# A retention layer's 24 input strips: value strips ahead of key and query strips

## The reference

```
z = h @ w_in                                   # 1024 -> 6144: q, k, v and gate of 4 heads
q = rope(z[q]); k = rope(z[k]) / 16            # 256 features a head
v, gate = z[v], z[gate]                        # 512 features a head
per chunk:  a = (q k^T) * decay;  o = a v + (q * q_dec) S;  S = c_dec * S + (k * k_dec)^T v
y = silu(gate) * groupnorm(o);  out = y @ w_out
```

## Time and profile before

| what | value |
|---|---|
| runs shown | 977.67, 977.97, 979.68 us; median 977.97 us |
| profiled execution, its own time | 976.55 us |
| its span | 974.3 us |
| mean granted TensorE clock | 0.995 of full speed |
| PE, PEld busy | 952.8, 883.3 us |
| DVE, ACT, POOL busy | 592.0, 430.1, 37.6 us |
| first to last transposition of values (L1089) | starts from 497.6 to 663.3 us |

### The profile page before, as it was taken

The page is one execution under the profiler, slowest core; times in us unless marked ns, Lnnn a source line. Parts: engine busy times, 40 slices in busy tenths (PEclk is TensorE's granted clock), DMA queues, the critical chain, the costliest instruction groups (busy, mean ns, idle before and its releaser), DMA issues. The chain is left out here.

```text
span 974.3 us, 17740 instructions
## 1 busy us (share of the span) xinstructions
PE 952.8 (98%) x7550; PEld 883.3 (91%) x7550; DVE 592.0 (61%) x768; ACT 430.1 (44%) x543; POOL 37.6 (4%) x68
## 2 busy tenths in 40 slices
PE   8999999899999999999999999999999999999996
PEld 8988998558999999999988978788899899999995
DVE  6866654874786653334875767676764875543443
ACT  6232224766554553333542644434344565543331
POOL 0510000000000000000001010000000000000000
PEclk9999999999999999999999999999999999999998
DMA  9987759967254445543556867675674344444411
GB/s 346 366 287 272 267 195 350 329 218 269 89 190 162 167 172 173 173 159 143 209 181 263 317 239 299 233 274 197 249 280 155 133 173 170 172 173 161 158 69 48
DMA packets 50989, 206.62 MB, mean 212 GB/s; under 512 B 3568, under 2 KB 3952, under 8 KB 35440
## 3 DMA queue, kind: packets, MB, share of 16 engines
q1 hardware_dynamic: 45504, 182.58, 52.7%
q0 software_dynamic: 5424, 23.15, 6.1%
HBM read 181.39 MB, written 24.33 MB: 211 GB/s over the span
## 5 line engine op out<-in xcount | busy, mean ns | idle before, releaser
L1289 ACT ACTIVATE wH<-raw 128x2048 fp32r<-128x2048 f32 x115 | 220.4, 1916 | 350.1 <-PE banks L630 339.6
L1669 DVE TENSOR_TENSOR wL<-raw,wH 128x2048 fp32r<-128x2048 f32 x112 | 256.6, 2291 | 191.0 <-ACT wH L1289 191.0
L628 PE MATMUL banks<-hH,wH 128*128 128x288 f32 x1152 | 346.0, 300 | 0.9 <-DVE sqacc L1754 0.5
L630 PE MATMUL banks<-hH,wL 128*128 128x288 f32 x1152 | 339.8, 295 | 0.0
L629 PE MATMUL banks<-hL,wH 128*128 128x288 f32 x1152 | 339.5, 295 | 0.0
L628 PEld LDWEIGHTS banks<-hH,wH 128*128 128x128 f32 x1152 | 217.7, 189 | 14.0 <-issue 10.5
L629 PEld LDWEIGHTS banks<-hL,wH 128*128 128x128 f32 x1152 | 216.8, 188 | 1.1 <-issue 0.7
L630 PEld LDWEIGHTS banks<-hH,wL 128*128 128x128 f32 x1152 | 216.5, 188 | 0.0
L630 PE MATMUL banks<-aH,wL 128*128 128x288 f32 x512 | 151.8, 296 | 0.0
L628 PE MATMUL banks<-aH,wH 128*128 128x288 f32 x512 | 151.3, 296 | 0.0
L629 PE MATMUL banks<-aL,wH 128*128 128x288 f32 x512 | 149.3, 292 | 0.0
(11 more groups left out here) (302 smaller groups left out, 1068.7 us busy)
## 6 DMA issues: line engine op xcount, KB each, us to landing
raw<-wst SPq DMA_DIRECT2D x119, 1024.0 KB, 4.9
cache_sb<-kcache SPq DMA_DIRECT2D x14, 1024.0 KB, 7.7
sslot<-state SPq DMA_DIRECT2D x11, 1024.0 KB, 5.9
sstate_out<-sslot POOLq DMA_DIRECT2D x11, 1024.0 KB, 5.5
raw<-vcache SPq DMA_DIRECT2D x6, 1024.0 KB, 10.6
w_area<-vcache SPq DMA_DIRECT2D x6, 1024.0 KB, 12.9
raw<-state SPq DMA_DIRECT2D x5, 1024.0 KB, 5.1
sstate_out<-raw POOLq DMA_DIRECT2D x5, 1024.0 KB, 5.4
```

Of the source, the lines that this page charges most:

```text
L628: nc.tensor.matmul(out[:, m, :], wH[:, u % 2, c], hi[:, k, :], start=first, stop=False)
L630: return nc.tensor.matmul(out[:, m, :], wL[:, u % 2, c], hi[:, k, :], start=False, stop=last)
L1289: nc.scalar.activation(wH[:, at % SPL, :], raw[:, raw_slot(at), :], ACT.Copy).then_inc(h_round, 1)
L1669: nc.vector.tensor_tensor(wL[:, at % SPL, :], raw[:, raw_slot(at), :], wH[:, at % SPL, :].bitcast(F32), ALU.subtract).then_inc(l_split, 1)
```

## The change

The order of the strips of heads 1, 2 and 3 becomes value, value, key, query. Head 0 keeps its order on PE, key, query, value, value, but DVE takes those four as p = 0, 2, 3, 1: the key, the two values, and then the query. `P_V_END`, which counts strips taken, and the two waits of PE for emptied banks (strips 4 and 5) follow. In the first four strips the head steps that do something (the clearing of `qpad`, `own_columns(0)`) and the split of strip 5 stay at the third and fourth place in DVE's order. Sizes, instructions and their number stay as they are.

```diff
 def _head_strips(h):
-    return 4 + h, h, 8 + 2 * h, 9 + 2 * h
+    values, turned = (8 + 2 * h, 9 + 2 * h), (4 + h, h)
+    return values + turned if h else turned + values
...
-P_V_END = (3, 7, 13, 19)
+
+
+FIRST_TAKEN = (0, 2, 3, 1)
+P_V_END = (2, 5, 11, 17)
...
-                pe.wait_ge(g_dve, GBUF + GD_RET + (p - 3 if p < 6 else p - 1))
+                pe.wait_ge(g_dve, GBUF + GD_RET + (1 if p == 4 else 4 if p == 5 else p - 1))
...
-            for p in range(N_RETIN):
+            for i, p in enumerate(FIRST_TAKEN + tuple(range(4, N_RETIN))):
                 s, c = S_RETIN + p, RET_ORDER[p]
-                head_step(p, 0)
-                head_step(p, 1)
+                if p >= 4:
+                    head_step(p, 0)
+                    head_step(p, 1)
                 dve.wait_ge(strip_used, s + 1)
...
-                    rotate(None, GD_RET + p, p, 16 + 2 * h + (c < NHR), lambda z: to[:, z:z + 1, :],
+                    rotate(None, GD_RET + i, p, 16 + 2 * h + (c < NHR), lambda z: to[:, z:z + 1, :],
                            at=s + SPL if p == 0 else None, src=pair(p) if p < 4 else G(p))
...
-                head_step(p, 2)
+                if i >= 3:
+                    head_step(i, 2)
                 if p == 2:
                     nc.vector.memset(qpad[:, :, :], 0.0).then_inc(r_dec, 1)
-                if p == 3:
-                    split_strip(s + 2, s + 2)
+                if i == 3:
+                    split_strip(S_RETIN + 5, S_RETIN + 5)
```

## The result

The changed kernel is slower: 984.38 us, median of 6 runs (982.90 to 984.78), against 978.25 us of the kernel before (6 runs, 976.71 to 979.68). The ratio is 1.0062, 95% interval 1.0052 to 1.0071. The forecast was 983.1, in a range of 980.0 to 985.6, slower with 0.86. The measured loss is 6.1 us, the forecast one 5.15.

A forecast was written before the change was run, and what follows sets the result against it. PE was taken to bound the kernel, with DVE's order deciding its waits at `kpad`. -0.54 + 1.60 + 2.84 + 1.25 = 5.15 us slower, on a median of 977.97, gave 983.1 us, range 980.0 to 985.6.

The forecast's parts named there:

- What bounds: PE, busy 952.8 of 974.3 us, bounds the kernel; only PE waits that go or come move the time.
- the sign: PE's idle time from 466 to 700 us grows by some 5 us; otherwise the prediction is wrong.
- The unit and the wait: On DVE, a rotation replacing a value strip adds 1.60 us; `own_columns` waiting directly behind the query's rotation adds 0.19.
- The four heads: Change in when PE gets `kpad`: head 0 gains 0.54 us; heads 1, 2, 3 lose 1.60, 2.84, 1.25.
- The clock: Rival: 2.9 us idle at head 3's `kpad` lowers PE's clock, up to 5 us more, 985 to 988; chance 0.08.
- The likeliest case: The forecast itself: DVE's order delays `kpad` in heads 1 to 3, 5.15 us slower, 983.1 us; chance 0.78.
- What was costed at nothing: ACT's high `kpad` copy (0.40 us a head), strips taken earlier, DMA queues and late splits add no time.
- That `kpad` is covered: Rival: DVE's chain has air, three value waits go and none replaces them, 2.89 us faster; chance 0.06.
- That DVE absorbs the rotations: Rival: DVE absorbs rotations of strips 7 and 12; only strips 13, 19 and waits count, about 0.7 us; chance 0.08.

The follow-up runs named there:

- the first head: Against the changed kernel, only DVE's order in head 0 stays changed; heads 1 to 3 return to key, query, value, value: 977.45 us against 977.38.
- its head alone: Three kernels against the one before, value strips first only in head 1, 2 or 3: single times 979.43, 980.32 and 979.71 us.
- the 6 matmuls: Changed kernel with 6 filling matmuls, results overwritten, ahead of PE's wait for `pad_low` in head 3: 981.75 us against 977.49 before.
- `pad_low` first: Changed kernel with `pad_low` directly behind `own_columns`, ahead of DVE's split of the next strip, in all heads: 980.49 us against 978.05 before.

## Why the prediction was right, point by point

*What bounds.* Right. All of the loss is in PE's idle time and clock. From 466 to 700 us before PE is idle for 4.7 us, and from 466 to 708 us after for 9.3, so the growth of some 5 us that was named as the sign is there; the slack of 0.54 us that was read between `pad_low` and `kpad`'s transpositions is the 0.52 that the first head gains.

*The unit and the wait.* In the changed trace the key strip of head 2 costs DVE 595.85 - 593.58 = 2.27 us, as reckoned. The step from a rotation to an instruction that waits for it is 0.59 us, against 0.37 without a wait: 0.22, and 0.19 was reckoned. DVE's rows (start us, us) in head 2:

```profile
607.50 0.45 DVE L1764 TENSOR_TENSOR qr<-sqacc 128x288 f32<-128x288 f32 x1
608.09 0.23 DVE L2053 TENSOR_TENSOR norms<-kr,norms 128x64 f32<-128x64 f32 x1
```

The Trainium skill ("VectorE: DVE Perf Modes", section "The DRAIN you can't avoid") has chained DVE instructions take the same time with a semaphore behind each as with one behind the last. Taken for waits, as the prediction takes it, it disagrees with these rows as it did with those of before. By it the sum would have been 4.8 us, by the traces it is 5.3.

*The four heads.* Reckoned -0.54, +1.60, +2.84, +1.25, together 5.15. Measured -0.52, +1.63, +2.87, +1.31, together 5.29, and each of the last three shown by itself with its head alone. That the strips taken earlier, ACT's copies and the DMA queues were put at nothing is borne out by what is left over, 0.14 us. The waits at `kpad` were forecast at 0.9, 1.9 and 2.9 us and are 1.02, 1.72 and 2.55.

*The clock.* This is the step that went otherwise. The likeliest case had no fall of the clock; the rival with it had 0.08. It falls in all four traces in which PE waits 2.5 us or more at `kpad`, and in none of the ten others. Its price is 1.58 us and not up to 5, since the fall does not last to the end of strip 20: in the changed kernel's trace the clock is back at 1.00 before 678 us. The rows named the danger (2.05 us kept the clock, a long idle stretch did not), and the chance given to it was too small. The 2.05 us row was also one execution: behind the same wait the clock fell in 8 of the 14 traces that there are now. So the number is in part luck. With the clock at its measured price the same sum would have been 5.15 + 1.58 = 6.7 us, or 984.7, which the range still held; the rival's own 985 to 988 us was too dear. The measured 6.1 us are in between 5.3 and 5.3 + 1.6 = 6.9, and the interval, 5.1 to 6.9 us, does not tell the two apart; the two traces without the fall in attention, 6.9 us apart, and the 6 matmuls do.

*What was costed at nothing.* One thing was missed beside the clock: the split of strip 20 is late by 0.50 us (PE's wait at L632), since the key's rotation is ahead of it. It ends before the wait for `kpad` does and costs nothing, but it is part of why that wait is 2.55 us and not 2.9. And ACT's copies are covered only as long as DVE's split stands beside them; with the split gone they are the next bound, as the ACT rows above show.

*The rivals.* That `kpad` is covered: no, the first head shows it alone. That DVE absorbs the rotations: no, heads 1 and 2 give 1.59 and 2.86 us.

## What to carry to other kernels

When a wait is to be removed, look at what the same engine waits for next and how much slack it has there: here 0.54 us stood behind a wait of 1.49, and that was all there was to win. Before an order is turned round, ask which of its members is dearest for the engine that must hand over (a rotation is 2.27 us on DVE, a value strip 0.67) and keep the dear ones away from the handing over. A long wait of PE can cost more than itself: here 2.55 us brought 1.6 us of low clock behind them. Put matmuls into it, if they end before the wait does, or end it sooner.

## What the runs showed of the hardware

The granted clock behind PE's waits among the retention strips: 1.00 behind 1.72 to 1.81 us at `kpad` in head 2 and behind 1.76 in head 3 (`pad_low` first), and at the 1.2 GHz level behind 2.54 to 2.56 us, in four traces of four, 1.56 to 1.63 us lost each time. Between them lies the 2.05 to 2.07 us wait in attention, which every kernel here has: behind it the clock fell in 8 of the 14 traces and stayed in 6, among them that of the kernel before. From the end of this wait to the group of matmuls at 478 us it takes 299.6 us where the clock stayed and 300.9 to 301.1 where it fell, so this fall costs 1.2 to 1.5 us. What decides there was not tried. Nor is the length of a wait all there is to it: every trace begins with PE waiting 2.6 to 2.9 us for a DMA, and the clock in the 8 us that follow is 1.00; what PE did ahead of the span no trace shows. "TensorE: Matmul & The Clock Gate", section "HAM oscillation", of the Trainium skill tells of such falls behind PE's waits for DMAs, and the traces here agree that one can follow a wait, with the numbers above.

One profiled execution of this kernel can thus be off by 1.2 to 1.5 us for a reason that lies 300 us from the change, which is why the steps were measured from a fixed instruction and not from the span.
